# Expert retrieval in a hybrid decoder block: a 65-pair top-16 search in place of 256 pairs, and nine fewer down products ahead of the slot transposes

## What is computed

```python
q = (ht @ w_query).reshape(N, PEER_HEADS, 2, PEER_QDIM // 2)
s1 = jnp.einsum('nhd,kd->nhk', q[:, :, 0], sub_keys_1)          # 128 scores
s2 = jnp.einsum('nhd,kd->nhk', q[:, :, 1], sub_keys_2)          # 128 scores
t1, i1 = lax.top_k(s1, 16)
t2, i2 = lax.top_k(s2, 16)
cand = t1[..., :, None] + t2[..., None, :]                      # 16 x 16 sums
sc, pos = lax.top_k(cand.reshape(N, PEER_HEADS, 256), 16)
eidx = the expert i1 * 128 + i2 at each of the 16 positions
gate = jax.nn.softmax(sc)
a = gelu(x . expert_down[eidx]);  y = sum(gate * a * expert_up[eidx])
```

## Time and profile before

| | us |
|---|---|
| median of 3 runs (lowest, highest) | 1532.32 (1531.72, 1532.43) |
| span of the profiled execution | 1528.9 |
| PE busy | 1507.2 (99%) |
| DVE busy | 1229.5 (80%) |
| ACT busy | 626.8 (41%) |
| POOL busy | 534.0 (35%) |

### The profile page before, as it was taken

How to read it: one execution, slowest core, us unless ns; L and a number is a source line. 1 busy time by engine, 2 the same in 40 slices (tenths; PEclk the granted TensorE clock), 3 DMA queues, 4 the chain that set the end, 5 groups by cost and what they waited for, 6 DMA issues and landing times.

```text
span 1528.9 us, 22605 instructions
## 1 busy us (share of the span) xinstructions
PE 1507.2 (99%) x8475; PEld 1344.2 (88%) x8475; DVE 1229.5 (80%) x2265; ACT 626.8 (41%) x1050; POOL 534.0 (35%) x357
## 2 busy tenths in 40 slices
PE   9999999999999999999999999999999999999997
PEld 6888888888899999998888888999999999999996
DVE  5577875449999999975676777888888889888885
ACT  6247565342222356662333333333333333333335
POOL 0323002055746710002111112555555556555530
PEclk9999999999999999999999999999999999999999
DMA  7302003323313568889899989999999999999971
GB/s 309 147 30 83 1 1 128 111 86 122 132 57 116 171 197 310 316 315 365 289 312 299 309 296 341 364 366 371 357 358 371 363 374 362 364 365 357 369 256 69
DMA packets 148509, 378.85 MB, mean 248 GB/s; under 512 B 11793, under 2 KB 76689, under 8 KB 145457
## 3 DMA queue, kind: packets, MB, share of 16 engines
q1 hardware_dynamic: 100400, 201.74, 38.1%
q0 software_dynamic: 37200, 138.56, 24.7%
q10 hardware_dynamic: 10800, 37.11, 6.6%
HBM read 338.50 MB, written 38.86 MB: 247 GB/s over the span
## 4 chain that ended last, share of the span: by engine, by line
PE 85%; DVE 10%; DMA 2%; ACT 1%; issue 1%; SPq 0%; ACTq 0%; DVEq 0%
PE bank L1900 22%; PE bank L1805 20%; PE bank L1524 12%; PE bank L1906 11%; PE bank L1814 10%; PE bank L1737 2%; DVE oh L1406 2%; DVE gp L1414 2%; DVE gp L1411 2%; DVE oh L1409 2%; PE bank L1721 1%; PE bank L1643 1%; DVE d_lo L1395 1%; DMA w_raw<-wts 1%; PE bank L1823 1%; PE bank L1641 1%
## 5 line engine op out<-in xcount | busy, mean ns | idle before, releaser
L1805 PE MATMUL bank<-h_hi,d_hi 128*128 128x384 f32 x1024 | 349.2, 341 | 1.1 <-DVE h_lo L1260 1.1
L1805 PE MATMUL bank<-h_lo,d_hi 128*128 128x384 f32 x1024 | 345.0, 337 | 0.0
L581 POOL DMA_INDIRECT p_in<-rows,p_row x128 | 160.2, 1251 | 404.1 <-DVE p_dot L1433 186.0
L581 POOL DMA_INDIRECT p_in<-up,p_row x128 | 172.0, 1344 | 190.7 <-DVE p_dot L1433 96.3
L1814 PE MATMUL bank<-h_hi,d_lo 128*128 128x384 f32 x1024 | 200.2, 338 | 0.0
L1805 PEld LDWEIGHTS bank<-h_hi,d_hi 128*128 128x128 f32 x1024 | 192.5, 188 | 4.0 <-issue 1.3
L1805 PEld LDWEIGHTS bank<-h_lo,d_hi 128*128 128x128 f32 x1024 | 192.4, 188 | 3.2
L1900 PE MATMUL bank<-u_hi,w_hi_e 128*128 128x512 f32 x750 | 192.3, 392 | 0.3 <-DVE w_lo_e L1458 0.3
L1900 PE MATMUL bank<-u_hi,w_lo_e 128*128 128x512 f32 x750 | 191.0, 390 | 0.0
L1906 PE MATMUL bank<-u_lo,w_hi_e 128*128 128x512 f32 x750 | 190.8, 390 | 0.0
L1814 PEld LDWEIGHTS bank<-h_hi,d_lo 128*128 128x128 f32 x1024 | 180.9, 188 | 0.0
(11 more groups left out here) (292 smaller groups left out, 2454.4 us busy)
## 6 DMA issues: line engine op xcount, KB each, us to landing
d_raw<-down SPq DMA_DIRECT2D x128, 512.0 KB, 5.8
u_raw<-up SPq DMA_DIRECT2D x128, 512.0 KB, 6.4
gates_dram<-ev ACTq DMA_DIRECT2D x12, 2048.0 KB, 6.8
g_e<-gates_dram SPq DMA_DIRECT2D x32, 768.0 KB, 9.8
w_raw<-wts SPq DMA_DIRECT2D x9, 2048.0 KB, 8.2
act_dram<-f_act ACTq DMA_DIRECT2D x59, 192.0 KB, 3.9
a_e<-act_dram SPq DMA_DIRECT2D x59, 192.0 KB, 5.8
xt<-x_in SPq DMA_DIRECT2D x2, 2048.0 KB, 11.8
```

The costliest lines, as they stand in the source:

```text
L581: pool.indirect_dma_start(out=p_in[n % GR][:], out_offset=None, in_=rows if kind == "D" else up.rearrange("n p d -> (n p) d"), in_offset=b ...
L1805: nc.tensor.matmul(bank[6 + e % 2][:, 0:TD], d_hi[e % DH_R][:, k], h[:, k, 0:TD], start=(k == j == 0), stop=False)
```

## The change

The 16 best of t1[i] + t2[j], with both lists sorted, lie among the pairs with (i + 1)(j + 1) <= 16. The change writes only rows that hold those, rounded up to 65 pairs: row 0 with 16 pairs, rows 1 and 2 with 8, rows 3 to 6 with 4, rows 7 to 14 with 2, row 15 with 1 (`RUNS`). The row of a found position is no longer its upper four bits: `posn` is compared with the starts of the rows (`is_ge`, a running count), and POOL's factors become differences of neighbouring key numbers, so that their sum is the key of the row. The column is `posn` and a mask, 15 shifted right by a quarter of the position's sixteenth. E_SLOTS falls from 33 to 24, with it E_DVE from 35 to 26 and NE from 59 to 50, and `POOL_KEYS` is another table.

```diff
--- before.py
+++ after.py
@@ -37,7 +37,7 @@
 
 E_AHEAD = 2
 E_REST = 2 * PH + E_AHEAD
-E_SLOTS = 33
+E_SLOTS = 24
 E_DVE = E_SLOTS + 2
 E_GATES = E_SLOTS + 4
 
@@ -55,7 +55,7 @@
 CMP_HIGH = {11: (0, 1, 2, 3), 12: (4, 5, 6), 13: (7, 8, 9)}
 CMP_LOW = {7: (0, 1), 8: (2, 3, 4), 9: (5, 6, 7), 10: (8, 9)}
 ROPED = {r + TB + 1: (r,) for r in range(3 * TB - 1)}
-POOL_KEYS = {6: 0, 8: 1, 11: 2, 13: 3, 16: 4, 20: 5, 25: 6}
+POOL_KEYS = {6: 0, 8: 1, 10: 2, 12: 3, 15: 4, 17: 5, 21: 6}
 DR = 4
 DH_R = 3
 UH = 3
@@ -63,6 +63,11 @@
 WARM = 14
 GR = 8
 PICKS = PH * TOPK
+
+
+RUNS = [(0, 1, 16), (1, 2, 8), (3, 4, 4), (7, 8, 2), (15, 1, 1)]
+PAIRS = sum(n * m for _, n, m in RUNS)
+ROW_STARTS = [sum(n * m for _, n, m in RUNS[:q]) + i * RUNS[q][2] for q in range(len(RUNS)) for i in range(RUNS[q][1])]
 
 
 def pick_order():
@@ -153,12 +158,13 @@
     xt = sb("xt", [P, TB, D])
     h_hi = sb("h_hi", [P, KC, T], F32R)
     h_lo = sb("h_lo", [P, KC, T], F32R)
-    cst = sb("cst", [P, 432])
+    cst = sb("cst", [P, 448])
     ident = cst[:, 0:P]
     cmp_neg = cst[:, 128:256].rearrange("p (q c) -> p q c", q=TB)
     cmp_vis = cst[:, 256:384].rearrange("p (q c) -> p q c", q=TB)
     inv_freq = cst[:, 384:416]
     iota16 = cst[:, 416:432]
+    starts = cst[:, 432:448]
     cstb = sb("cstb", [P, 384], BF16)
     ident_b, mask_b = cstb[:, 0:P], cstb[:, P:384]
     prm = sb("prm", [P, 96])
@@ -255,8 +261,13 @@
 
 
     at[0] = after_w
-    cand = sb("cand", [P, TB, TOPK, TOPK])
-    candw = sb("candw", [P, TB, TOPK * TOPK])
+    cand = sb("cand", [P, TB, 72])
+    candw = sb("candw", [P, TB, 72])
+    dif = [sb(f"dif{r}", [P, TB, TOPK]) for r in range(2)]
+    quart = sb("quart", [P, TB, TOPK], U32)
+    mask = sb("mask", [P, TB, TOPK], U32)
+    fifteen = sb("fifteen", [P, TB, TOPK], U32)
+    at[0] = after_w + 8192
     hit_0 = [sb(f"hit0{s}", [P, TB, TOPK, TOPK]) for s in range(2)]
     assert at[0] == after_w + 16384
     q_sb = [sb(f"q_sb{i}", [P, T]) for i in range(2)]
@@ -639,7 +650,7 @@
 
             act.dma_start(prm[:], params).then_inc(S("prm_loaded"), 16)
             act.dma_start(posi[:], pos).then_inc(S("freq_loaded"), 16)
-            act.dma_start(cst[:, 384:432], consts[:, 384:432]).then_inc(S("freq_loaded"), 16)
+            act.dma_start(cst[:, 384:448], consts[:, 384:448]).then_inc(S("freq_loaded"), 16)
             act.wait_ge(S("pool_set"), 1)
             nc.scalar.activation(rt[:], warm[:, 0:TB], ACT.Copy)
             act.wait_ge(S("prm_loaded"), 16)
@@ -1325,6 +1336,7 @@
                     last = V.max_index(idx[b][:, 8:16], vals[b][:, 8:16], tmp[b])
                 return last
 
+            link(V.memset(fifteen[:], TOPK - 1))
             top_count = [0]
             for hd in range(PH):
                 r = hd % 2
@@ -1340,25 +1352,35 @@
                           [src[:, b * NK:(b + 1) * NK] for b in range(TB)],
                           [work[s][:, b] for b in range(TB)]).then_inc(S("s_free"), 1)
                 dve.wait_ge(S("s_free"), 2 * hd + 2)
-                for b in range(TB):
-                    V.tensor_tensor(cand[:, b], tv[r][0][:, b].unsqueeze(2).broadcast_to([P, TOPK, TOPK]),
-                                    tv[r][1][:, b].unsqueeze(1).broadcast_to([P, TOPK, TOPK]), ALU.add)\
-                     .then_inc(S("cand_done"), 1)
-                dve.wait_ge(S("cand_done"), TB * (hd + 1))
+                for q, (first, n, m) in enumerate(RUNS):
+                    at_q = ROW_STARTS[first]
+                    V.tensor_tensor(cand[:, :, at_q:at_q + n * m].rearrange("p b (i j) -> p b i j", j=m),
+                                    tv[r][0][:, :, first:first + n].unsqueeze(3).broadcast_to([P, TB, n, m]),
+                                    tv[r][1][:, :, 0:m].unsqueeze(2).broadcast_to([P, TB, n, m]), ALU.add)\
+                     .then_inc(S("pair_step"), 1)
+                dve.wait_ge(S("pair_step"), 9 * hd + 5)
                 link(top16([score[:, b, hd] for b in range(TB)], [posn[:, b] for b in range(TB)],
-                           [cand[:, b].rearrange("p i j -> p (i j)") for b in range(TB)],
-                           [candw[:, b] for b in range(TB)]))
-                V.tensor_copy(tif[r][0][:], ti[r][0][:])
+                           [cand[:, b, 0:PAIRS] for b in range(TB)],
+                           [candw[:, b, 0:PAIRS] for b in range(TB)]))
+                V.tensor_scalar(quart[:], posn[:], 4, None, ALU.logical_shift_right).then_inc(S("pair_step"), 1)
+                V.tensor_copy(dif[r][:], ti[r][0][:]).then_inc(S("pair_step"), 1)
                 V.tensor_copy(tif[r][1][:], ti[r][1][:])
-                V.tensor_scalar(pab[r][0][:], posn[:], 4, None, ALU.logical_shift_right)
-                link(V.tensor_scalar(pab[r][1][:], posn[:], TOPK - 1, None, ALU.bitwise_and))
+                dve.wait_ge(S("pair_step"), 9 * hd + 6)
+                V.tensor_tensor(mask[:], fifteen[:], quart[:], ALU.logical_shift_right).then_inc(S("pair_step"), 1)
+                dve.wait_ge(S("pair_step"), 9 * hd + 7)
+                V.tensor_copy(tif[r][0][:, :, 0:1], dif[r][:, :, 0:1])
+                V.tensor_tensor(tif[r][0][:, :, 1:TOPK], dif[r][:, :, 1:TOPK], dif[r][:, :, 0:TOPK - 1], ALU.subtract)
+                dve.wait_ge(S("pair_step"), 9 * hd + 8)
+                V.tensor_tensor(pab[r][1][:], posn[:], mask[:], ALU.bitwise_and).then_inc(S("pair_step"), 1)
+                dve.wait_ge(S("pair_step"), 9 * hd + 9)
                 if hd >= 2:
                     dve.wait_ge(S("key_done"), 2 * (hd - 1))
                 for s in range(2):
                     V.tensor_tensor(hit[r][s][:].rearrange("p b k r -> p (b k) r"),
-                                    pab[r][s][:].rearrange("p b k -> p (b k)").unsqueeze(2)
+                                    (pab[r][1] if s else posn)[:].rearrange("p b k -> p (b k)").unsqueeze(2)
                                     .broadcast_to([P, TB * TOPK, TOPK]),
-                                    iota16.unsqueeze(1).broadcast_to([P, TB * TOPK, TOPK]), ALU.is_equal)\
+                                    (iota16 if s else starts).unsqueeze(1).broadcast_to([P, TB * TOPK, TOPK]),
+                                    ALU.is_equal if s else ALU.is_ge)\
                      .then_inc(S("hit_eq"), 1)
                 if hd >= 1:
                     keys_of(hd - 1)
@@ -1928,7 +1950,7 @@
 
 def constants():
 
-    c = np.zeros((P, 432), np.float32)
+    c = np.zeros((P, 448), np.float32)
     c[:, 0:P] = np.eye(P)
     t = np.arange(T).reshape(TB, P).T
     vis = np.zeros((P, TB, CP), np.float32)
@@ -1937,6 +1959,7 @@
     c[:, 256:384] = vis.reshape(P, -1)
     c[:, 384:416] = np.float32(10000.0) ** (-np.arange(HALF, dtype=np.float32) / np.float32(HALF))
     c[:, 416:432] = np.arange(TOPK)
+    c[:, 432:448] = ROW_STARTS
     b = np.zeros((P, 384), np.dtype("bfloat16"))
     b[:, 0:P] = np.eye(P)
     q, k = np.arange(P)[:, None], np.arange(P)[None]
```

## The result

The changed kernel takes 1534.84 us (median of 13 runs, 1534.58 to 1536.01); the kernel before, in its 13 runs beside it, 1531.20. The ratio is 1.0023, 95% interval 1.0015 to 1.0031. The profiled execution has a span of 1532.8 us, 3.9 more than before.

The account below looks back on a forecast made before the run. PE, busy 99% of the span, was taken as the bound, with DVE pacing the gate phase. Terms of 9.5, 1.0, 1.1 and 0 made 11.6 us on 1532.3: 1543.9 us, range 1536 to 1548.

Parts of the forecast that it names:

- When PE arrives: Slot transposes: with nine blocks left out ahead of them, PE could start them at 508.19 us.
- DVE's work for a head: DVE's key search and its steps: 19.2 us a head, 4.3 less than before; head 7's sums at 488.9 at the earliest.
- What is in the way: Head 7 on DVE: sums and comparisons wait for whole POOL instructions, so the gates are ready at 517.6, not 505.8.
- usual waits: Rival, head 7's sums beside POOL: they lose 2 us, not 10; PE waits 0 to 2; 1534.4 to 1537; chance 0.11.
- Term 1: Slot transposes: PE waits 9.5 us for the gates, and everything behind shifts.
- Term 2: After PE's wait: the nine transposes run at half pace, 1.0 us more, bounds 0 and 5.
- Term 3: Up phase: nine blocks moved there cost 0.125 us more each than early, 1.1 us in all.
- Term 4: Early stretch: fewer GELU stores and loads and fewer d_lo on POOL give 0, since PE never waits for them.
- The base: Time of the kernel before, 1532.3 us, to which the forecast added its 11.6 us.
- faster: Rival, up phase: gathers get more room, some 76 experts gain up to 9.5 us; 1524 with DVE in time; chance 0.03.

Follow-up runs that it names:

- E_SLOTS 27: Changed kernel with three more down products ahead of the slot transposes (E_SLOTS 27 instead of 24, NE 53): 1525.93 us, 0.9962 of the kernel before.
- the run with mixed `u` tiles: Kernel before with one group of up-phase tiles (u2, u3, u_hi2, w_hi_e, w_lo_e, a_e, p_in) shifted by 64 bytes: 1533.40 us, ratio 1.0014.

## Why the prediction was wrong, step by step

- **When PE arrives** (508.19): right. Its last matmul there starts at 508.69; this trace ran about 0.7 us later as a whole.
- **DVE's work for a head.** The search over 65 columns, 3.5: measured 503.23 - 499.73 = 3.50. The small ones, 0.95: 0.90. The two products at L1317, 2.3: 2.27. The sums of head 7 at 488.9 at the earliest: they came at 493.43. The forecast let PE's scores pace DVE at heads 1 to 7; in the trace DVE waits for them once more than before, 4.13 us at 359.38, and not in the later heads. Beside POOL the five sums took 4.96 us for head 1, and 2.92, 2.84 and 2.13 for heads 3, 4 and 6, where I had put in 0.75. Head 7's came 4.5 us late, more than the two that the forecast allowed for. That changed nothing, since POOL's run lasted longer still; but three of the five sums paid for it and not all five, and they took 6.3 us, not some 10.
- **What is in the way**: right. Sums done 499.2 forecast, 499.70 measured; comparisons done 508.2 and, with the next instruction's start, 508.62; gates 517.6 and 518.01. I had both comparisons behind the d_lo; the first slipped ahead, the second paid. The run without POOL's d_lo tested the cause. The rule of the Trainium skill (SBUF — State Buffer, "Who interferes with whom") on which the forecast leaned against the "usual waits" held. The rival "usual waits", 1534.4 to 1537, met the time by luck: PE waited 9.04 us, not 0 to 2.
- **Term 1**, 9.5 us: 9.04 (9.37 from start to start).
- **Term 2**, 1.0 us: the nine transposes lost 0.9. Five matmuls behind them lost another 0.7, most of which PE's shorter gaps in the gate phase gave back (3.5 us waited there, 4.1 in the run that had no wait ahead). By the medians, terms 1 and 2 together are worth 8.9 (against E_SLOTS 27), where they were forecast at 10.5 and the trace's own parts come to about 10; the rest is not placed.
- **Term 3**, 1.1 us: **this is the step that failed.** It carried 8.36 us an expert over from the trace of before, for the nine blocks and, by leaving them out of the sum, for the 69 that were in the up phase already. The changed kernel runs at 8.27. At that pace the nine blocks cost 9 x (8.27 - 4.08 - 4.16) = 0.3, and, what weighs more, each of the 69 became 0.09 cheaper too. The cause is the 64 bytes by which the widened `cst` moves the tiles: moving them back costs 7.4 us.
- **Term 4**, 0: the profile shows no wait of PE on these.
- **The base.** The sum was set on the 1532.32 of three runs; thirteen gave 1531.20. In the changed kernel's profiled execution span and time lie 1.8 us apart (1532.8 and 1534.58), not the forecast's 3.4.

These are the parts of the miss: 1543.9 - 1534.84 = 9.1, of which 7.4 is the layout, 1.1 the base, and 0.6 the sum of all other terms.

The number that gave the effect away was in the forecast: it found that an up-phase expert is 0.125 us slower than its two parts, and the rival "faster" priced its loss at up to 9.5 us. It had nearly the right size (7.4 measured) and the wrong cause. I refuted the cause (full DMA engines) with the window at a share of 0.63, correctly, and then took the pace for a constant, at a chance of 0.03 for a change. A pace that is higher than the sum of its parts and that no resource explains is an unknown, not a constant. And the 16 new columns move every tile behind them, for which the forecast has no term.

## What to carry to other kernels

Ahead of counting instructions, list what a change does to addresses: a widened tile near the start moves all that follow, and here 64 bytes were worth 5 us, and the search at the old place of the transposes nothing. When a stage's time is not the sum of its parts, find out what the rest is before building on it; padding one allocation is a cheap experiment. And as long as POOL works without a gap, short two-input DVE operations beside it wait for a POOL instruction each, whatever their width (2.4 us for sums that take 0.2 alone), so an estimate must count operations there and not columns.

## What the runs showed of the hardware that I had not expected

PE's pace in back-to-back matmuls depends on where tiles stand in SBUF, in steps as small as 32 bytes (down tiles at 96 or 64: 8.36 or 8.32): with the same instructions, data and granted clock and nearly the same DMA share, a step of a down product takes 173.3 ns or alternates between 174 and 179, and a step of an up product 226.7 or up to 236. It also depends on the stage around the matmuls: with d at 96 and h at 0 the down products are even ahead of the up phase, uneven between up products from tiles at 64, and even between up products from tiles at 0. In the Trainium skill, SBUF — State Buffer, section "Who interferes with whom", PE has one read port for the moving operand and an independent one for the weights. Moving the weights d alone, with h left at 0, changed the pace by up to 1% (8.36, 8.32, 8.27), and in the run with mixed `u` tiles a moving tile at 64 against weights at 0 cost 3% of a step (233 ns for 227). Whether the two ports hinder each other there, which would go against the page, or something else that reads or writes the moved tiles is behind it, no run here shows.

The lower clock came after a pause of PE as short as 2.4 us: in the run without POOL's d_lo the granted clock is 0.50 at the transposes and they take 421 ns, as they do after 9 us, where they take 272 without a pause.
